# Forgetting attention: every low part of the exponentials on GpSimd, with one count for them

## The reference

```python
s = jnp.einsum("bhqd,bhkd->bhqk", qb, kb) * scale
s = s + log_forget_cum[:, :, qs:qe, None] - log_forget_cum[:, :, None, :qe]
mask = jnp.arange(qs, qe)[:, None] >= jnp.arange(qe)[None, :]
p = jax.nn.softmax(jnp.where(mask, s, -jnp.inf), axis=-1)
outs.append(jnp.einsum("bhqk,bhkd->bhqd", p, v[:, :, :qe]))
```

## Time and profile before

| what | value |
|---|---|
| median of three runs | 2602.05 us |
| the profiled execution: its time, its span | 2598.46 us, 2596.3 us |
| PE busy | 2433.0 us, 94% |
| DVE busy | 1418.0 us, 55% |
| ACT busy | 948.2 us, 37% |
| POOL busy | 557.8 us, 21% |
| mean granted TensorE clock | 0.958 |

### The profile page before, as it was taken

One profiled execution on the slowest core, in us unless ns is written; L12 is line 12 of the kernel. 1 busy time (PEld: TensorE's weight loads), 2 busy tenths in 40 slices (PEclk: granted clock), 3 DMA queues, 4 the chain that ended last, 5 costly groups with the idle time before them and its releaser, 6 DMA issues. The chain is left out here.

```text
span 2596.3 us, 37171 instructions
## 1 busy us (share of the span) xinstructions
PE 2433.0 (94%) x14204; PEld 2152.8 (83%) x14204; DVE 1418.0 (55%) x2006; ACT 948.2 (37%) x1578; POOL 557.8 (21%) x655
## 2 busy tenths in 40 slices
PE   6999999999959999978999998999998999999999
PEld 6899999999958888976777777888876888887887
DVE  7665655565456567544666662111466666655553
ACT  5333333333344445432444443111334333334332
POOL 0023300000023344231444444222310333000000
PEclk8999999999979999987998998999999999999999
DMA  4365632565230000010000002111433566326653
GB/s 183 121 209 196 209 114 95 214 227 188 101 130 1 26 26 0 1 33 7 7 7 4 3 1 81 48 49 41 163 113 104 180 221 232 133 87 255 211 197 111
DMA packets 125908, 281.13 MB, mean 108 GB/s; under 512 B 9456, under 2 KB 56432, under 8 KB 122432
## 3 DMA queue, kind: packets, MB, share of 16 engines
q1 hardware_dynamic: 125760, 279.10, 31.0%
HBM read 198.60 MB, written 80.33 MB: 107 GB/s over the span
## 5 line engine op out<-in xcount | busy, mean ns | idle before, releaser
L1068 DVE TENSOR_TENSOR f_w_lo<-f_rw,f_w_hi 128x1024 fp32r<-128x1024 f32 x154 | 203.1, 1319 | 218.7 <-ACT f_w_hi L590 218.6
L833 PE MATMUL f_ps<-u_hi,f_w_hi 128*128 128x260 f32 (+1 forms) x1056 | 283.9, 323 | 26.5 <-DVE f_w_lo L1068 13.6
L833 PE MATMUL f_ps<-u_hi,f_w_lo 128*128 128x260 f32 (+1 forms) x1056 | 282.4, 322 | 0.0
L833 PE MATMUL f_ps<-u_lo,f_w_hi 128*128 128x260 f32 (+1 forms) x1056 | 282.4, 322 | 0.0
L590 ACT CAST f_w_hi<-f_rw 128x1024 fp32r<-128x1024 f32 x154 | 161.3, 1047 | 165.1 <-PE f_ps L833 148.7
L833 PE MATMUL f_ps<-f_far_hi,f_w_hi 128*128 128x260 f32 (+1 forms) x792 | 211.8, 322 | 8.7 <-DVE f_ev L1084 8.7
L833 PEld LDWEIGHTS f_ps<-u_hi,f_w_hi 128*128 128x128 f32 x1056 | 178.0, 192 | 43.1 <-DVE f_w_lo L1068 15.4
L833 PE MATMUL f_ps<-f_far_lo,f_w_hi 128*128 128x260 f32 (+1 forms) x792 | 210.9, 321 | 0.0
L833 PE MATMUL f_ps<-f_far_hi,f_w_lo 128*128 128x260 f32 (+1 forms) x792 | 210.8, 321 | 0.0
L833 PEld LDWEIGHTS f_ps<-u_lo,f_w_hi 128*128 128x128 f32 x1056 | 177.7, 191 | 14.2
L833 PEld LDWEIGHTS f_ps<-u_hi,f_w_lo 128*128 128x128 f32 x1056 | 177.6, 191 | 14.1
(11 more groups left out here) (385 smaller groups left out, 5987.1 us busy)
## 6 DMA issues: line engine op xcount, KB each, us to landing
f_rw<-in_gu SPq DMA_DIRECT2D x88, 512.0 KB, 4.4
f_rw<-kept_dsum SPq DMA_DIRECT2D x32, 704.0 KB, 4.9
f_rw<-kept_hid SPq DMA_DIRECT2D x33, 520.0 KB, 5.7
f_rw<-in_down SPq DMA_DIRECT2D x24, 704.0 KB, 4.1
f_rw<-kept_hid SPq DMA_DIRECT2D x33, 512.0 KB, 5.5
f_gt_raw<-in_gate SPq DMA_DIRECT2D x24, 512.0 KB, 3.5
h_in<-in_wd SPq DMA_DIRECT2D x11, 1024.0 KB, 7.2
kept_dsum<-h_in SPq DMA_DIRECT2D x44, 256.0 KB, 3.1
```

The lines of the kernel that those rows point to most:

```text
L833: last = nc.tensor.matmul(out[:, b, 0:N], w[:, c], u[:, b * N:(b + 1) * N], start=(j < 3 and k == 0 and i == 0), stop=(k == 3 and i == 2), ...
L1068: nc.vector.tensor_tensor(slot(w_lo, st), src, slot(w_hi, st).bitcast(F32), ALU.subtract).then_inc(wlo_done, 1)
```

## The change

All 28 low parts of a pair are POOL's. DVE's subtraction goes, with its wait for its own cast. The two counts become one, `plo_done`, of 28 per pair, and each pair of waits becomes one wait for it.

```diff
-LO_DVE = 4
-def lo_counts(units_done):
-    return units_done - units_done // LO_DVE, units_done // LO_DVE
...
-        def wait_split(eng, p, units_done):
-            by_pool, by_dve = lo_counts(units_done) if units_done > 0 else (0, 0)
-            wait(eng, plo_pool, p, LO_P, by_pool)
-            wait(eng, plo_dve, p, LO_V, by_dve)
...  (pool)
                 for w in range(PW):
-                    if w % LO_DVE == LO_DVE - 1:
-                        continue
                     n = ST_UNITS[w % NW][4]
                     wait(pool, phi_done, p, PW, w + 1)
                     nc.gpsimd.tensor_tensor(p_lo[:, w % 3, 0:n], p32[:, w % 3, 0:n], p_hi[:, w % 3, 0:n].bitcast(F32),
-                                            ALU.subtract).then_inc(plo_pool, 1)
+                                            ALU.subtract).then_inc(plo_done, 1)
...  (scalar)
-                            wait_split(act, p, 0)
+                            wait(act, plo_done, p, PW, 0)
...
-                    wait_split(act, p, w - 2)
+                    wait(act, plo_done, p, PW, w - 2 if w >= 2 else 0)
...  (tensor)
-                    wait_split(pe, p, w + 1)
+                    wait(pe, plo_done, p, PW, w + 1)
...  (vector)
                     nc.vector.tensor_copy(p_hi[:, w % 3, 0:n], p32[:, w % 3, 0:n]).then_inc(phi_done, 1)
-                    if w % LO_DVE == LO_DVE - 1:
-                        wait(dve, phi_done, p, PW, w + 1)
-                        nc.vector.tensor_tensor(p_lo[:, w % 3, 0:n], p32[:, w % 3, 0:n],
-                                                p_hi[:, w % 3, 0:n].bitcast(F32), ALU.subtract).then_inc(plo_dve, 1)
```

More of the change, by code:

```diff
@@ L1644, in fox_attention_phase @@
                                                                     sem("mhi_done"), sem("m_done"))
-        st_ready, exp_done, phi_done, plo_pool, plo_dve, pv_done = (sem("st_ready"), sem("exp_done"),
-                                                                    sem("phi_done"), sem("plo_pool"),
-                                                                    sem("plo_dve"), sem("pv_done"))
+        st_ready, exp_done, phi_done, plo_done, pv_done = (sem("st_ready"), sem("exp_done"), sem("phi_done"),
+                                                           sem("plo_done"), sem("pv_done"))
         ln_done, rden_done, o_done = sem("ln_done"), sem("rden_done"), sem("o_done")
@@ L1650, in fox_attention_phase @@
         PW, PM = 2 * NW, 2 * NM
-        LO_P, LO_V = lo_counts(PW)
-        def wait_split(eng, p, units_done):
-            by_pool, by_dve = lo_counts(units_done) if units_done > 0 else (0, 0)
-            wait(eng, plo_pool, p, LO_P, by_pool)
-            wait(eng, plo_dve, p, LO_V, by_dve)
         W_HI_AT, W_LO_AT = [2, 5, 8, 11, 14, 17], [4, 7, 10, 13, 16, 19]
```

## The result

The changed kernel's median is 2604.48 us over 20 runs (2595.72 to 2613.30), the one before has 2598.10 us over 20 runs (2588.20 to 2606.52). The ratio is **1.0027, 95% interval 1.0016 to 1.0037**: slower by 7 us, 4 to 10. Twelve more runs in a later series gave 1.0019 (1.0006 to 1.0032), 5 us. The forecast was +11.1 us: the right way, but too large.

What follows compares the result with a forecast made beforehand. It took the sum of DVE and POOL, which exclude each other, as the bound. 3 x 2.9 + 2.4 = +11.1 us on the profiled 2598.46 gives 2609.6; the median lies 3.59 higher: 2613 us, range 2603.5 to 2621.

Steps and rivals of the forecast that it cites:

- What bounds: In the pairs' weighing stretch, DVE and POOL exclude each other, so the sum of the two bounds, not one engine.
- The account: Per pair, 6.33 us added to POOL less 3.57 removed from DVE: 2.76 us more, 11.0 for four pairs.
- Units 7 and 8: POOL's start of unit 8 comes later: 1.27 us for a 0.54 tail, plus one hand-over, +0.8 us a pair.
- Units 15 to 20: Units 15 and 19 dearer on POOL, +1.04 together, with two hand-overs +1.2 us a pair; 0.7 in the last.
- Units 23 and 27: Unit 23: 1.27 us for a 0.55 tail and a hand-over, +0.8; unit 27, the last, +0.1 a pair.
- Units 3 and 11: Both low parts have slack ahead of their weighings, so moving them to POOL costs 0.
- The waits: Each weighing and exponential loses one of two waits; at most 2 us in all comes back, taken as 0.
- The clock: Longer idle moments may bring falls costing up to 1.7 us each; none in the sum, up to six in the range.
- rival B: Stalls grow and three to six clock falls come with them: +18 to +21 us, about 2621; chance 0.12.
- The sign on the casts: The prediction is wrong if DVE's casts beside POOL's work take their free time; no size given.
- A: The ring takes most up, casts for later units slip in between: +4 to +5.5 us, about 2607; chance 0.20.
- C: DVE's queue is freed, casts pass before POOL's next unit, POOL gets a stock: -8 us, 2594; chance 0.03.

Runs made afterwards that it cites:

- second profile: Profile from the repeat of the changed kernel with no edit, beside the kernel before; that repeat's median 2603.89 us, ratio 1.0019.
- held casts: Changed kernel, but DVE casts units 8, 16, 20, 24 only after POOL's low part of the unit before; 2609.91 us, 1.0038 to the kernel before.
- only the small units moved: Against the kernel before, only units 3, 11, 15 and 27 go to POOL, 7, 19 and 23 stay on DVE; 2603.34 us, ratio 1.0014.

## Why the prediction came out too large

**What bounds.** Right. Taking POOL's share away gives time back, putting more on DVE gives more, and what the change costs in the stretches at equal clock lies between units 5 and 27 of the pairs.

**The account, 11.0 us.** It is an account of durations, and a duration is not a hold. A 512-wide cast takes 0.41 us alone but kept POOL for 0.14 to 0.21. Two ways of working out that agree don't support each other when both take the same durations.

**The step that failed** is the price of what stands around a moved unit: "1.27 us on POOL stand where the tail of 0.54 stood: +0.73, and about 0.1 for one more hand-over", with "the weights' low part and the cast stay, on either side of it". It lets both DVE instructions keep their whole duration and adds a hand-over, and it was used at all four places. With the subtraction gone from DVE's queue, the instruction behind it is issued while POOL works, and only what is left of it holds POOL up:

| POOL's start of unit | DVE's work around the moved unit, before | after |
|---|---|---|
| 8 (pair 2 of the second profile) | weights 0.68, cast 0.41 and hand-over | 0.45 and 0.36; order as predicted |
| 16 | 0.29 from the subtraction's end | none; the cast ends 0.9 us before POOL ends unit 15 |
| 20 (pairs 1 to 3) | 1.02 from the subtraction's end | 0.41 and 0.36; order as predicted |
| 24 | 0.36 from the subtraction's end | 0.13; the cast ends 1.15 us before POOL ends unit 23 |

So at units 16 and 24 the cast doesn't stay behind the moved unit. At units 8 and 20 it does, but it is cheaper. (In pair 4 of the second profile unit 8's cast runs ahead too.) The held casts are the test: with them the time is +10 us (6 to 14) over the kernel before.

**Units 7 and 8, +0.8 a pair.** Measured at full clock +0.5 from unit 5 to 14 (last pair +0.3).

**Units 15 to 20, +1.2 (last pair 0.7).** Measured +0.5 (1.0 in the last pair, where I had seen more room than there was; why was not followed up).

**Units 23 and 27, +0.9.** Measured +0.4 (last pair +0.1). 1.27 us for a tail of 0.55 still holds (+0.72), but the 0.36 us from the subtraction's end to POOL's start of unit 24 are down to 0.13: that makes +0.5. By these durations the cast and the hand-over that never came make 0.3 of the 0.5 that is missing; held, the cast brought back only 0.17. The rest is open. In the last pair the stretch was 7.04 us long before the change.

**Units 3 and 11, nothing.** Right: at equal clock units 0 to 5 are not longer (7.21 for 7.32 us), and with only the small units moved, units 5 to 14 are within 0.1 us of before in pairs 2 to 4.

Together 3 x 1.4, and 0.3 + 1.0 + 0.1 in the last pair, make 5.6 us if pair 2 stands for the first three; the four pairs of the second profile add up to 4.4, those of the first to 5.9. Measured are 7 (4 to 10) and 5 (2 to 8).

**The waits, 0.** Right. **The clock, 0 on average.** Right within about 1.5 us, though the first profile had three long falls, as rival B had it.

**The signs.** Pair 1 was to be near 35 us, and it was (35.27), but by luck: some 2.5 us of its growth lie among units 0 to 5, where the granted clock is 0.50 for 0.76, and units 5 to 27 grow by 0.6. POOL's 26 to 27 us busy came true. POOL's start of unit 8 after its end of unit 6 grew by 0.5, not 0.8, and that of unit 24 after unit 22 from 0.91 to 1.34, by 0.4. The sign on the casts could not catch the error: beside POOL's work the casts of units 22 to 24 do take 0.86, 0.60 and 0.53 us instead of their free 0.41 and 0.36, but what counts is what POOL loses by them.

**Rivals.** A gave +4 to +5.5, and with the size it has the case; its reason, casts that slip in between, is the one the runs showed at units 16 and 24. C saw the same freed queue but priced it as the whole effect; it takes away about half of the predicted cost instead. The chances don't add up as written: 0.57 + 0.12 - 0.10 is 0.59 for slower, and 0.38 for same.

## What to carry to other kernels

When two engines exclude each other, as here, the price of an instruction on one of them is what it keeps the other from doing, not its own duration. Read it from how much longer the other's instruction becomes beside it (here 0.14 to 0.21 us for a cast of 0.41). Before you add a moved instruction to a chain, ask which instruction behind it in the old queue can now be issued earlier: its price falls to what is left of it when the other engine comes free, and it can pass ahead of the moved work. Where single executions differ by more than the change, compare stretches at the same granted clock, pair by pair; totals of waits need the same clock too.

## What the runs showed that I had not expected

Among the runs of one kernel a straight line through time against mean granted clock falls by 1.5 us for each 0.001 of clock, over all eleven kernels together; alone, the held casts don't show it (their line is flat). In one series the executions of the kernel before spread from 0.951 to 0.965 in this clock and from 2587 to 2610 us. Of 32 runs of the changed kernel 7 are below 2600.0 us, the mean of the one before. Within a pair the change of stretch from profile to profile lies among the first units (7.1 to 9.7 us from unit 0 to 5), where the granted clock falls; from unit 14 on the same kernel repeats to 0.1 us.
